# First units of block 1: q's and k's weights in halves, modulation sums rearranged, extra matmuls on TensorE

## The chip, the cores and the metric

The kernel runs on one core of one Trainium2 chip. The metric is device time in microseconds (us) of one execution; the kernel before takes 1196.93 us (median of three runs).

## The reference, cut to what matters

Two transformer blocks on 256 tokens of width 1024, all in float32. The change lies in the first 100 us, in the head of block 1:

```python
mod = jax.nn.silu(c) @ w_ada + b_ada                 # (1024) @ (1024, 6144)
sh1, sc1, ga1, sh2, sc2, ga2 = jnp.split(mod, 6)
h = modulate(rms_norm(x, g_norm1), sh1, sc1)         # h * (1 + sc1) + sh1
z = h @ w_in                                         # (256, 1024) @ (1024, 5120)
q, k, v, xb, bg, cg, gates = jnp.split(z, splits)
```

Behind it come rotary attention, a gated convolution, output rows, a mixture of 32 experts, and a second block.

## The kernel before

**Products.** Each matrix is split in two float32r parts, a lead (ScalarE: copy) and a rest (original minus lead), and every product is three matmuls: lead x lead, lead x rest, rest x lead. `row_products` issues such a triple for one of 8 contraction tiles k of 128 rows, for 128 tokens and 512 columns. A unit such as `q0` is 8 triples (24 matmuls) in one PSUM bank. `channel_tiles` makes the units of xb, cg and bg: 16 triples of 256 tokens.

**Weights.** A weight chunk (2 MB: 8 contraction tiles x 512 columns) comes by DMA into one of six ring slots. SyncE (SP) issues all of them in the order of `loads1`, and waits before each for the unit that last used the slot (`holds`). ScalarE then writes the leads in two halves of 2048 elements a partition (`lead_weights`, L1550), VectorE the rest of the first half (`rest_weights`, L1992), GpSimd the rest of the second half in two quarters (L814). GpSimd's queue runs through the chunks in order, and issues eleven small loads (`small_loads`) behind v's rests.

**Head.** c is turned into columns (`cT`). The modulation sums g1a and g1b are each 2 halves of 16 matmuls over 2 MB of `w_ada` (`modulation_half`, L902): g1a gives shift and scale for contraction tiles 0 to 3, g1b for 4 to 7. ScalarE copies the sums (`modulation_sums`, L1599), TensorE makes columns of them (`half_columns`, L947 and L948, 8 matmuls of 2 moving columns), ScalarE copies these (L1614), VectorE makes the scales (`first_scales`). Beside it, x is squared (L1559), VectorE forms the row factors and writes xn (L2038), and TensorE transposes xn (L892). Then h is made by contraction tile: `h1_fulls` (L2076) and `h1_rests` (L2085) on VectorE, `h1_leads` (L1620) on ScalarE; q's products follow.

**Late sums.** g2 (4 chunks of 2 MB, `late_pair`, L912, all in slot 4) follows behind the units named in `PAIR_AT`; each chunk's load waits for the sum before it. VectorE and ScalarE work strictly in program order: VectorE forms the rests of k and v, then `head_norm` of q (L1931 to L1949), adds g2_1, forms xb's rest, adds g2_2, then `head_norm` of k, whose transposes (`tk`, L959) TensorE needs behind xb1. ScalarE adds g2_0 (L1599) ahead of v's leads, and writes xb's leads before it copies v0 out.

Of the kernel before, what the change touches and what calls it, by code (L numbers as in the profile page):

```python
# [13 lines left out]
P = 128  # L14
# [26 lines left out]
COL = 512  # L41
# [92 lines left out]
def two_blocks(nc, A, consts, out):  # L134
    with ExitStack() as ctx:
# [179 lines left out]
        dense_order = ["g1a", "g1b"] + UNITS1 + [f"pa{t}{h}" for t, h in TH] + [f"pb{t}{h}" for t, h in TH]  # L315
# [20 lines left out]
        PAIR_AT = {"q1": ("g2", 0), "k1": ("g2", 1), "v1": ("g2", 2), "xb1": ("g2", 3)}  # L336
        PAIR_AT.update({f"gate{n}0": ("g3", n) for n in range(4)})
        ROW_AT = {"cg0": 4, "cg1": 5, "bg0": 10, "bg1": 11}
# [4 lines left out]
        small_order = ["cT", "params", "xt00", "xt10", "cols_g1a", "xt01", "xt11", "cols_g1b"]  # L343
# [51 lines left out]
        dense_released = {"g1a": (sem("acc_copied"), 1), "g1b": (sem("acc_copied"), 2)}  # L395
# [24 lines left out]
        small_released = {"cT": (sem("c_ready"), 1), "params": (sem("pcol_ready"), 1), "rsb": (sem("rsb_ready"), 1),  # L420
# [85 lines left out]
        def ada_half(group, n, slot):  # L506

            loads = []
            for at, c in enumerate(ADA_GROUPS[group]):
                src = w_ada[4 * n * P:4 * (n + 1) * P, c * COL:(c + 1) * COL].rearrange("(k p) n -> p k n", p=P)  # L510
                loads.append((four_of(slot)[:, :, at * COL:(at + 1) * COL], src))
            chunk(f"{group}_{n}", slot, loads, after(group) if n else (sem("ada_pairs"), 1 + (group == "g1b")))
# [11 lines left out]
        def columns_in(name):  # L524
            slot = ROT1[ROT_NAMES.index(name) % 3]
            weights(name, slot, [(wide(slot), cols(w_in, IN1[name] * COL))], name + "1")
# [3 lines left out]
        columns_in("q")  # L530
        ada_half("g1b", 0, 4)
        ada_half("g1b", 1, 0)
        columns_in("k")
# [140 lines left out]
        def halves(m):  # L674

            size, slot = split_size[m], slot_of[split_chunks[m]]
            out = []
            for a in range(0, size, HALF_SLOT):
                b = min(a + HALF_SLOT, size)
                out.append((ring[:, slot, a:b], ring_r[:, slot, a:b], lead_home(m)[1][:, a:b]))  # L680
            return out

        lead_done = [0]
        for m in range(len(split_chunks)):
            lead_done.append(lead_done[-1] + len(halves(m)))

        ON_DVE = {M[name] for name in ("q", "fk", "fv", "hi", "hg", "gate_b0")}
        rest_dve, rest_pool = [0], [0]
        for m in range(len(split_chunks)):
            rest_dve.append(rest_dve[-1] + 1 + (m in ON_DVE))  # L690
            rest_pool.append(rest_pool[-1] + (0 if m in ON_DVE else 2 * (len(halves(m)) - 1)))

# [31 lines left out]
        def _(sp_):  # L724
# [5 lines left out]

            sp_.dma_start(cst[:, 0:C_FIRST], consts[:, 0:C_FIRST]).then_inc(sem("first_in"), 16)
            for name in loads1:
                load(name)
# [3 lines left out]
                if name == "g1a_0":  # L737
                    sp_.dma_start(x[:, :, :], A["x"][0].rearrange("(t p) d -> p t d", p=P)).then_inc(sem("x_in"), 16)
# [52 lines left out]
        def _(pool):  # L791
# [15 lines left out]
            def rest_weights(m):  # L807

                if len(halves(m)) == 2 and m not in ON_DVE:
                    w, rest, lead = halves(m)[1]  # L810
                    pool.wait_ge(sem("w_lead"), lead_done[m + 1])
                    for a in (0, HALF_SLOT // 2):
                        b = a + HALF_SLOT // 2
                        nc.gpsimd.tensor_tensor(rest[:, a:b], w[:, a:b], lead[:, a:b].bitcast(F32),  # L814
                                                ALU.subtract).then_inc(sem("w_rest_b"), 1)
# [18 lines left out]
        def _(pe):  # L834
# [8 lines left out]
            def weights_ready(m, at):  # L843

                if at < HALF_SLOT or m in ON_DVE:
                    pe.wait_ge(sem("w_rest_a"), rest_dve[m] + 1 + (at >= HALF_SLOT))
                else:
                    pe.wait_ge(sem("w_rest_b"), rest_pool[m] + 1 + (at >= HALF_SLOT + HALF_SLOT // 2))
# [180 lines left out]

            pe.wait_ge(sem("first_in"), 16)  # L1030
# [6 lines left out]
            pe.wait_ge(sem("params_in"), 16 * (len(PARAM_ROWS) - 1))  # L1037
            o = small.claim(pe, "params")
            nc.tensor.transpose(o[:, 0:PARAM_N], prow[0:PARAM_N, :], ident[0:PARAM_N, 0:PARAM_N]).then_inc(small.done, 1)
            modulation_half("g1a", 1, g1a).then_inc(dense.done, 1)  # L1040

            def h1_ready(t, k):
                return sem("h1_rest"), KD * (k // 4) + 4 * t + k % 4 + 1

            for t, h in XT:
                pe.wait_ge(sem("xn_ready"), t + 1)
                transposes(f"xt{t}{h}", xn[:, t, :], h)
                if (t, h) == (1, 0):
                    half_columns("g1a")
            g1b = dense.claim(pe, "g1b")  # L1050
            q_rows = [dense.claim(pe, f"q{t}") for t in range(TT)]
            for k in range(4):
                row_products(q_rows[0], M["q"], 0, k, h1_ready)
            modulation_half("g1b", 0, g1b).then_inc(sem("ada_pairs"), 1)
            for k in range(4):
                row_products(q_rows[1], M["q"], 1, k, h1_ready)
                if k == 1:
                    modulation_half("g1b", 1, g1b).then_inc(dense.done, 1)
            half_columns("g1b")
            for t in range(TT):  # L1060
                for k in range(4, KD):
                    last = row_products(q_rows[t], M["q"], t, k, h1_ready)
                last.then_inc(dense.done, 1)

            for name in UNITS1:
                chunk_name, u = name[:-1], int(name[-1])
                if chunk_name == "q":
                    pass
                elif chunk_name in ("xb", "cg", "bg"):
# [428 lines left out]
        def _(act_):  # L1498
# [44 lines left out]
            def lead_weights(m, parts=(0, 1)):  # L1543

                if 0 in parts:
                    arrived(act_, split_chunks[m])
                    act_.wait_ge(*lead_holds(m))
                for n, (w, _, lead) in enumerate(halves(m)):
                    if n in parts:
                        af(lead, w, ACT.Copy).then_inc(sem("w_lead"), 1)  # L1550
# [36 lines left out]
            af(pcol[:, :], src[:, 0:PARAM_N], ACT.Copy).then_inc(sem("pcol_ready"), 1)  # L1587
# [35 lines left out]
            modulation_sums("g1a")  # L1623
            normed_columns(0, 0)
            normed_columns(1, 0)
            half_columns(0)
            lead_weights(0, (0,))
            h1_leads(0, 0)
            normed_columns(0, 1)
            normed_columns(1, 1)  # L1630
            h1_leads(1, 0)
            lead_weights(0, (1,))
            act_.wait_ge(sem("lb_sub_ready"), 1)
            af(lbt[:, 2:4, :], lbt[:, 0:2, :], ACT.Exp).then_inc(sem("lb_exp_ready"), 1)
            modulation_sums("g1b")
            half_columns(1)
            h1_leads(0, 1)
            h1_leads(1, 1)

            for unit in UNITS1:  # L1640
                name, u = unit[:-1], int(unit[-1])
                if u == 0:
                    lead_weights(M[name] + 1)
# [107 lines left out]
            for unit in UNITS2:  # L1751
                name, u = unit[:-1], int(unit[-1])
                if u == 0 and name != "fq":
                    lead_weights(M[name] + 1, (1,) if name == "hq" else (0, 1))
# [128 lines left out]
        def _(dve):  # L1883
# [101 lines left out]
            def rest_weights(m, parts=(0, 1)):  # L1985

                for n in range(2 if m in ON_DVE else 1):
                    if n not in parts:
                        continue
                    w, rest, lead = halves(m)[n]  # L1990
                    dve.wait_ge(sem("w_lead"), lead_done[m] + 1 + n)
                    v.tensor_tensor(rest, w, lead.bitcast(F32), ALU.subtract).then_inc(sem("w_rest_a"), 1)  # L1992
# [47 lines left out]
            def lower_bounds_differences():  # L2040
                dve.wait_ge(sem("pcol_ready"), 1)
# [19 lines left out]
            def first_scales(h):  # L2061
# [3 lines left out]
                dve.wait_ge(sem("pcol_ready"), 1)  # L2065
# [21 lines left out]

            first_scales(0)
            h1_fulls(0, 0)
            rest_weights(0, (0,))  # L2090
            h1_rests(0, 0)
            h1_fulls(1, 0)
            h1_rests(1, 0)
            lower_bounds_differences()
            rest_weights(0, (1,))
            lower_bounds()
            link(v.tensor_copy(rs[:, 9, :], rs[:, 0, :]))
            first_scales(1)
# [501 lines left out]
```

## Time and profile before

| | |
|---|---|
| runs | 1193.87, 1196.93, 1198.81 us; median 1196.93 |
| profiled execution, span | 1196.8 us |
| TensorE busy, share of the span | 96% |
| mean granted TensorE clock | 0.989 |
| DMA over the span | 277 GB/s |
| DMA from 359 to 718 us (the experts) | about 421 GB/s |

The profiled execution has no time of its own beside its span, which stands 0.1 us from the median. A busy TensorE is not one at full speed: at half the granted clock each matmul lasts about twice as long, and the expert stage keeps it busy at the pace of its transfers.

### The profile page before, as it was taken

What the parts mean: (1) busy time and instruction counts of PE and PEld (TensorE: products, weight loads), DVE (VectorE), ACT (ScalarE), POOL (GpSimd) and SP (SyncE); (2) the same over time, 40 slices, a digit from 0 to 9 for tenths busy, and PEclk for the clock granted to TensorE, in tenths of its full rate; (3) what the DMA queues carried; (4) which work ended last, traced back from release to release, by engine and by line L of the source; (5) the groups of instructions that cost most, each with busy time, mean ns of one, the idle gap of its engine ahead of it and who ended that gap; (6) DMA issues with size and microseconds to landing.
All of it is one profiled execution on the core that took longest, in us unless ns stands there. A gap on an engine that the chain in (4) does not pass through costs nothing.

```text
span 1196.8 us, 15588 instructions
## 1 busy us (share of the span) xinstructions
PE 1148.5 (96%) x5930; PEld 761.6 (64%) x5930; DVE 481.1 (40%) x971; ACT 410.5 (34%) x609; POOL 222.0 (19%) x100
## 2 busy tenths in 40 slices
PE   4999999999999999999989998999999999999998
PEld 2678867774444444444434435978877788888886
DVE  3475552753222222222212215589454653323226
ACT  3533454232111111111111115664245363444334
POOL 0163333300000000000000002200313444443522
PEclk8899999999999999999999998999999999999999
DMA  9897366689899999999999996453223464645541
GB/s 355 322 329 264 128 229 246 269 329 367 339 377 421 423 422 421 422 422 422 422 420 421 422 421 240 160 192 126 86 71 141 150 194 159 210 147 181 201 163 48
DMA packets 92329, 331.68 MB, mean 277 GB/s; under 512 B 3937, under 2 KB 26754, under 8 KB 66674
## 3 DMA queue, kind: packets, MB, share of 16 engines
q1 hardware_dynamic: 91648, 330.36, 71.2%
q0 software_dynamic: 432, 0.48, 0.2%
q8 instruction: 40, 0.66, 0.2%
q14 instruction: 15, 0.12, 0.0%
q10 hardware_dynamic: 194, 0.06, 0.0%
HBM read 329.84 MB, written 1.05 MB: 276 GB/s over the span
## 4 chain that ended last, share of the span: by engine, by line
PE 73%; DMA 16%; DVE 6%; issue 2%; ACT 2%; SPq 0%; DVEq 0%; ACTq 0%
DMA ring<-in_w 15%; PE ps L839 14%; PE ps L840 13%; PE ps L841 13%; PE ps L1196 13%; PE ps L1238 5%; PE ps L1168 1%; PE ps L1169 1%; DVE ring_r L1992 1%; PE ps L912 1%; DMA ring<-in_w_ada 1%; ACT ring_r L1550 1%; PE ps L1349 1%; PE ps L976 1%; PE ps L974 1%
## 5 line engine op out<-in xcount | busy, mean ns | idle before, releaser
L814 POOL TENSOR_TENSOR ring_r<-ring,ring_r 128x1024 fp32r<-128x1024 f32 x76 | 197.8, 2623 | 824.5 <-ACT ring_r L1550 824.4
L1196 PE MATMUL ps<-ring,arena 128*64 128x512 f32 x1008 | 226.0, 596 | 8.8 <-DMA ring<-in_w 7.7
L840 PE MATMUL ps<-ring_r,hl_r 128*128 128x512 f32 x528 | 211.4, 400 | 0.0
L839 PE MATMUL ps<-ring_r,hl_r 128*128 128x512 f32 x480 | 197.5, 411 | 10.7 <-DVE hr_r L2085 6.1
L841 PE MATMUL ps<-ring_r,hr_r 128*128 128x512 f32 x480 | 192.0, 400 | 0.0
L1550 ACT ACTIVATE ring_r<-ring 128x2048 fp32r<-128x2048 f32 x90 | 167.4, 1907 | 62.5 <-PE ps L841 45.0
L1196 PEld LDWEIGHTS ps<-ring,arena 128*64 128x64 f32 x1008 | 69.5, 137 | 149.0 <-issue 127.6
L1992 DVE TENSOR_TENSOR ring_r<-ring,ring_r 128x2048 fp32r<-128x2048 f32 x52 | 121.3, 2339 | 84.5 <-ACT ring_r L1550 84.3
L839 PEld LDWEIGHTS ps<-ring_r,hl_r 128*128 128x128 f32 x480 | 91.8, 191 | 41.2 <-issue 14.7
L840 PEld LDWEIGHTS ps<-ring_r,hl_r 128*128 128x128 f32 x528 | 101.0, 191 | 21.9
L841 PEld LDWEIGHTS ps<-ring_r,hr_r 128*128 128x128 f32 x480 | 91.8, 191 | 22.3
L1238 PE MATMUL ps<-ring,arena 128*64 128x512 f32 x448 | 100.9, 604 | 0.7 <-ACT arena L1715 0.7
L1715 ACT ACTIVATE arena<-ps 128x512 f32<-128x512 f32 x16 | 9.6, 598 | 185.1 <-PE ps L1224 185.1
L1238 PEld LDWEIGHTS ps<-ring,arena 128*64 128x64 f32 x448 | 31.3, 138 | 59.1 <-issue 57.3
L1721 ACT ACTIVATE hl_r<-hl 128x512 fp32r<-128x512 f32 x32 | 20.1, 630 | 119.4 <-DVE hl L2307 119.4
L1168 PE MATMUL ps<-arena_r,ya_r 128*128 128x128 f32 x256 | 60.2, 280 | 0.5 <-DVE flagf L2260 0.5
L1168 PEld LDWEIGHTS ps<-arena_r,ya_r 128*128 128x128 f32 x256 | 49.2, 192 | 13.6 <-issue 13.5
L2293 DVE COPY arena<-ps 64x1 f32<-64x1 f32 x32 | 5.0, 156 | 121.8 <-PE ps L1204 121.3
L2307 DVE SCALAR_TENSOR_TENSOR hl<-ps,arena,ga2b 128x512 f32<-128x512 f32 x32 | 23.9, 748 | 68.9 <-PE ps L1238 68.9
L2300 DVE TENSOR_TENSOR arena<-arena,ps 128x512 f32<-128x512 f32 x16 | 11.0, 688 | 92.9 <-PE ps L1196 92.9
L839 PE MATMUL ps<-hl_r,ring_r 128*128 128x256 f32 x160 | 45.8, 286 | 0.0
L840 PE MATMUL ps<-hr_r,ring_r 128*128 128x256 f32 x160 | 45.1, 282 | 0.0
(370 smaller groups left out, 1650.7 us busy)
## 6 DMA issues: line engine op xcount, KB each, us to landing
ring<-in_w SPq DMA_DIRECT2D x91, 2048.0 KB, 21.5
ring<-in_w_in SPq DMA_DIRECT2D x21, 2048.0 KB, 8.4
ring<-in_w_ada SPq DMA_DIRECT2D x16, 1024.0 KB, 10.2
ring<-in_w_ffn_gate SPq DMA_DIRECT2D x11, 1024.0 KB, 5.2
ring<-in_w_ffn_up SPq DMA_DIRECT2D x11, 1024.0 KB, 7.8
ring<-in_w_ffn_down SPq DMA_DIRECT2D x5, 2048.0 KB, 7.8
ring<-in_w_ada SPq DMA_DIRECT2D x4, 2048.0 KB, 8.7
ring<-in_w_o SPq DMA_DIRECT2D x2, 2048.0 KB, 7.7
```

The lines of the kernel that those rows point to most:

```text
L814: nc.gpsimd.tensor_tensor(rest[:, a:b], w[:, a:b], lead[:, a:b].bitcast(F32), ALU.subtract).then_inc(sem("w_rest_b"), 1)
L839: mm(o, lhsT=a_lead, rhs=b_lead, start=start, stop=False, skip_group_check=True)
L840: mm(o, lhsT=a_lead, rhs=b_rest, start=False, stop=False, skip_group_check=True)
L841: return mm(o, lhsT=a_rest, rhs=b_lead, start=False, stop=stop, skip_group_check=True)
L912: last = mm(o[32 * i:32 * i + 32, :], lhsT=cpad[:, 2 * n + k, :], rhs=w[:, k, i * COL:(i + 1) * COL], start=start and k == 0, stop=stop an ...
L1168: mm(into, lhsT=xp_l[:, t, k, :], rhs=S_r[:, t, :], start=t == 0, stop=False)
L1196: last = mm(H[slots_of(e), :], lhsT=xs[:, k, slots_of(e)], rhs=w, start=k == 0, stop=k == KD - 1)
L1238: last = mm(Y[slots_of(e), :], lhsT=hidT[:, f, slots_of(e)], rhs=w2_rows(e, f, half, early), start=f == 0, stop=f == FT - 1)
L1550: af(lead, w, ACT.Copy).then_inc(sem("w_lead"), 1)
L1721: af(ys_l[:, cols_], ys[:, cols_], ACT.Copy).then_inc(sem("moe_ys_lead"), 1)
L1992: v.tensor_tensor(rest, w, lead.bitcast(F32), ALU.subtract).then_inc(sem("w_rest_a"), 1)
L2307: v.scalar_tensor_tensor(ys[:, cols_], Y, place_w, ga2b[:, cols_], ALU.mult, ALU.mult).then_inc(sem("moe_ys_scaled"), 1)
```

## The change

- SP: x is loaded ahead of everything but the small table. q's and k's chunks are split; their first halves (contraction tiles 0 to 3) are issued between the 1 MB pieces of g1b_0 (q upper, piece, k upper, piece). Then come g1b_1, q's second half, k's second half.
- Leads: q's are written in quarters, k's in halves of their own. q's rests are four quarters on VectorE; k's first half goes to GpSimd, its second half to VectorE.
- TensorE: 9 matmuls without use (`keep_warm`, float32, 128x256) behind `cT`; the transposes of xn stand before g1a_0 (one unit) and before g1a_1 (three units); `half_columns` of g1a follows g1a_1; then 3 more `keep_warm`; the first halves of q0 and q1; g1b_0; first half of k0; g1b_1; two triples of k1; `half_columns` of g1b; the rest of k1's first half; q's second halves; g2_0; k's second halves.
- g2_1 to g2_3 stand behind v0, xb0 and cg0 (before: k1, v1, xb1), the rows of `modulation_row` one unit later.
- VectorE adds g2_1 behind xb's rest, g2_2 behind cg's rest, g2_3 in the attention loop.

```diff
-        PAIR_AT = {"q1": ("g2", 0), "k1": ("g2", 1), "v1": ("g2", 2), "xb1": ("g2", 3)}
+        PAIR_AT = {"q1": ("g2", 0), "v0": ("g2", 1), "xb0": ("g2", 2), "cg0": ("g2", 3)}
...
+            if m == M["q"]:
+                return [(a, a + QUARTER, "dve") for a in range(0, SLOT, QUARTER)]
+            if m == M["k"]:
+                return [(0, QUARTER, "pool"), (QUARTER, HALF_SLOT, "pool"), (HALF_SLOT, SLOT, "dve")]
...
             sp_.dma_start(cst[:, 0:C_FIRST], consts[:, 0:C_FIRST]).then_inc(sem("first_in"), 16)
+            sp_.dma_start(x[:, :, :], A["x"][0].rearrange("(t p) d -> p t d", p=P)).then_inc(sem("x_in"), 16)
             for name in loads1:
-                load(name)
+                if name == "g1b_0":
+                    upper_half("q")
+                    (view, src), second = chunks[name]
+                    sp_.dma_start(view, src).then_inc(chunk_in[slot_of[name]], 16)
+                    upper_half("k")
+                    sp_.dma_start(*second).then_inc(chunk_in[slot_of[name]], 16)
+                else:
+                    load(name)
...
+            def keep_warm(n):
+
+                for _ in range(n):
+                    mm(dense.bank("k0")[:, 0:C_FIRST], lhsT=ident, rhs=cst[:, 0:C_FIRST], start=True, stop=True)
...
+            keep_warm(9)
+            pe.wait_ge(sem("params_in"), 16 * (len(PARAM_ROWS) - 1))
+            o = small.claim(pe, "params")
+            nc.tensor.transpose(o[:, 0:PARAM_N], prow[0:PARAM_N, :], ident[0:PARAM_N, 0:PARAM_N]).then_inc(small.done, 1)
+            normed_transposes(XT[0:1])
             pe.wait_ge(sem("cpad_ready"), 1)
             g1a = dense.claim(pe, "g1a")
             modulation_half("g1a", 0, g1a).then_inc(sem("ada_pairs"), 1)
...
+            normed_transposes(XT[1:])
             modulation_half("g1a", 1, g1a).then_inc(dense.done, 1)
...
+            half_columns("g1a")
+            keep_warm(3)
             q_rows = [dense.claim(pe, f"q{t}") for t in range(TT)]
...
+            for t in range(TT):
+                half_rows(q_rows[t], "q", t, 0)
+            g1b = small.claim(pe, "g1b")
             modulation_half("g1b", 0, g1b).then_inc(sem("ada_pairs"), 1)
...
+            k_rows = [dense.claim(pe, f"k{t}") for t in range(TT)]
+            half_rows(k_rows[0], "k", 0, 0)
+            modulation_half("g1b", 1, g1b).then_inc(small.done, 1)
+            for k in range(2):
+                row_products(k_rows[1], M["k"], 1, k, h1_ready)
             half_columns("g1b")
+            for k in range(2, 4):
+                row_products(k_rows[1], M["k"], 1, k, h1_ready)
             for t in range(TT):
...
+                half_rows(q_rows[t], "q", t, 1).then_inc(dense.done, 1)
+            late_pair(*PAIR_AT["q1"])
+            for t in range(TT):
+                half_rows(k_rows[t], "k", t, 1).then_inc(dense.done, 1)
```

## Rows read from the trace of the kernel before

**Rows 1.** The page, part 1: busy time of the engines.
```profile
PE 1148.5 (96%) x5930; PEld 761.6 (64%) x5930; DVE 481.1 (40%) x971; ACT 410.5 (34%) x609; POOL 222.0 (19%) x100
```

**Rows 2.** Windows of 10 us: busy us of each engine, granted clock, DMA share, GB/s.
```profile
40.00:50.00 10.00, 7.51 (x32) 6.28 (x31) 5.61 (x19) 6.63 (x11) 0.00 (x0) 0.66 1.03 399
60.00:70.00 10.00, 10.00 (x52) 6.73 (x51) 9.48 (x16) 1.62 (x3) 10.00 (x9) 1.00 0.89 308
110.00:120.00 10.00, 10.00 (x82) 9.53 (x81) 4.97 (x15) 4.84 (x7) 0.00 (x0) 1.00 0.60 209
```

**Rows 3.** Windows of 1 us, the same columns: where clock and DMA change.
```profile
15.00:16.00 1.00, 0.00 (x0) 0.00 (x0) 0.73 (x5) 0.26 (x3) 0.00 (x0) 0.89 1.05 387
...
22.00:23.00 1.00, 1.00 (x9) 1.00 (x8) 0.00 (x0) 0.73 (x2) 0.00 (x0) 0.70 1.05 387
...
26.00:27.00 1.00, 0.00 (x0) 0.00 (x0) 0.71 (x3) 1.00 (x3) 0.00 (x0) 0.51 1.05 387
...
32.00:33.00 1.00, 1.00 (x5) 0.76 (x3) 0.61 (x1) 0.46 (x2) 0.00 (x0) 0.58 1.05 385
...
43.00:44.00 1.00, 0.00 (x0) 0.00 (x0) 0.78 (x4) 0.45 (x2) 0.00 (x0) 0.54 1.02 406
...
49.00:50.00 1.00, 1.00 (x4) 0.81 (x3) 1.00 (x1) 1.00 (x1) 0.00 (x0) 0.54 1.05 387
...
52.00:53.00 1.00, 1.00 (x9) 0.54 (x7) 0.00 (x0) 0.00 (x0) 1.00 (x1) 1.00 0.04 16
```

**Rows 4.** Timeline of TensorE, 0 to 100 us: start, us, line, what, idle before and releaser.
```profile
9.40 3.37 PE L902 MATMUL ps<-ring,cpad 128*32 128x512 f32 x16 [6.16 <-DMA ring<-in_w_ada]
...
17.37 3.64 PE L902 MATMUL ps<-ring,cpad 128*32 128x512 f32 x16 [4.36 <-DMA ring<-in_w_ada]
20.95 1.88 PE L892 MATMUL ps<-cst,ya 128*128 128x128 f32 x8
...
29.10 0.79 PE L839 MATMUL ps<-ring_r,hl_r 128*128 128x512 f32 x1 [3.66 <-DVE hr_r L2085]
...
37.23 1.92 PE L902 MATMUL ps<-ring,cpad 128*32 128x512 f32 x16
...
44.92 0.80 PE L839 MATMUL ps<-ring_r,hl_r 128*128 128x512 f32 x1 [2.48 <-DVE hr_r L2085]
...
52.98 1.92 PE L912 MATMUL ps<-ring,cpad 128*32 128x512 f32 x16
...
66.27 1.92 PE L912 MATMUL ps<-ring,cpad 128*32 128x512 f32 x16
...
81.55 0.38 PE L839 MATMUL ps<-hl_r,ring_r 128*128 128x256 f32 x1
...
95.67 1.09 PE L959 MATMUL ps<-cst,arena 128*128 128x128 f32 x8 [1.47 <-DVE arena L1949]
```

**Rows 5.** Timeline of ScalarE: first square, one lead half, xb's leads.
```profile
11.94 0.63 ACT L1559 ACTIVATE spp<-x 128x512 f32<-128x512 f32 x1 [8.23 <-DMA x<-in_x]
...
24.61 1.91 ACT L1550 ACTIVATE ring_r<-ring 128x2048 fp32r<-128x2048 f32 x1
...
69.57 3.73 ACT L1550 ACTIVATE ring_r<-ring 128x2048 fp32r<-128x2048 f32 x2 [2.60 <-DMA ring<-in_w_in]
```

**Rows 6.** Timeline of VectorE: xn, rest of q's first half, head_norm of q begins.
```profile
17.71 1.42 DVE L2038 TENSOR_SCALAR ya<-x,rs 128x1024 f32<-128x1024 f32 x2
...
26.55 2.29 DVE L1992 TENSOR_TENSOR ring_r<-ring,ring_r 128x2048 fp32r<-128x2048 f32 x1 [0.28 <-ACT ring_r L1550]
...
59.61 3.42 DVE L1931 TENSOR_TENSOR spp<-arena 128x1024 f32<-128x1024 f32 x1
```

**Rows 7.** Timeline of GpSimd: v's quarters, xb's quarters.
```profile
59.25 6.04 POOL L814 TENSOR_TENSOR ring_r<-ring,ring_r 128x1024 fp32r<-128x1024 f32 x2 [3.79 <-ACT ring_r L1550]
...
73.39 5.75 POOL L814 TENSOR_TENSOR ring_r<-ring,ring_r 128x1024 fp32r<-128x1024 f32 x2 [0.37 <-ACT ring_r L1550]
```

**Rows 8.** Timeline of SP: issue of g2_1's load; xb's follows it.
```profile
54.96 0.88 SPq L729 DMA_DIRECT2D ring<-in_w_ada  x2
```

More of the change, by code:

```diff
@@ L672, in chunk_done @@
             return (sem("down_chunks"), int(name[4:]) + 1) if name != "down5" else after("down11")
[L674 to L680, printed above, removed]
-            return out
-        lead_done = [0]
+        QUARTER = HALF_SLOT // 2
+        ON_DVE = {M[name] for name in ("fk", "fv", "hi", "hg", "gate_b0")}
@@ L688, in two_blocks, with lead_of @@
[L688 to L691, printed above, removed]
+            for n, (_, _, by) in enumerate(rest_pieces(m)):
+                rested[by] += 1
+                rest_at[m, n] = sem(dict(dve="w_rest_a", pool="w_rest_b")[by]), rested[by]
+        def lead_of(m, b):
+            return sem("w_lead"), lead_at[m, [n for n, (_, end) in enumerate(lead_pieces(m)) if b <= end][0]]
@@ L807, in rest_weights @@
             def rest_weights(m):
[L809 to L815, printed above, removed]
+                for a, b, by in rest_pieces(m):
+                    if by == "pool":
+                        w, rest, lead = piece(m, a, b)
+                        pool.wait_ge(*lead_of(m, b))
+                        nc.gpsimd.tensor_tensor(rest, w, lead.bitcast(F32), ALU.subtract).then_inc(sem("w_rest_b"), 1)
             for m in range(M["fq"]):
@@ L1541, in two_tiles, with lead_weights @@
                 return t[:, 2 * u:2 * u + 2, :]
[L1543 to L1550, printed above, removed]
+            led = [0]
+            def lead_weights(m, parts=None):
+                for n in range(len(lead_pieces(m))) if parts is None else parts:
+                    a, b = lead_pieces(m)[n]
+                    if split_chunks[m] in upper_halves and b <= HALF_SLOT:
+                        act_.wait_ge(sem(f"{split_chunks[m]}_upper_in"), 16)
+                    else:
+                        arrived(act_, split_chunks[m])
+                    if n == 0:
+                        act_.wait_ge(*lead_holds(m))
+                    led[0] += 1
+                    assert lead_at[m, n] == led[0]
+                    w, _, lead = piece(m, a, b)
+                    af(lead, w, ACT.Copy).then_inc(sem("w_lead"), 1)
             squares = [0]
@@ L1983, in pair, with rest_weights @@
                 return src.rearrange("p (j t) -> p j t", t=T)
[L1985 to L1992, printed above, removed]
+            rests = [0]
+            def rest_weights(m, parts=None):
+                for n, (a, b, by) in enumerate(rest_pieces(m)):
+                    if by == "dve" and (parts is None or n in parts):
+                        rests[0] += 1
+                        assert rest_at[m, n][1] == rests[0]
+                        w, rest, lead = piece(m, a, b)
+                        dve.wait_ge(*lead_of(m, b))
+                        v.tensor_tensor(rest, w, lead.bitcast(F32), ALU.subtract).then_inc(sem("w_rest_a"), 1)
             def gated_a(tag, t, h):
```

153 lines of the change are left out of this document (84 added, 69 removed).

## The prediction

> **What bounds the kernel now.** I read first the busy times, then windows over the head of block 1, then TensorE's timeline and what released it, then the queues beside it. TensorE is busy 96% of the span [rows 1], so a gain must come from where it idles or runs at half clock. In the head it does both: between 40 and 50 us it is busy 7.51 of 10 us at a mean clock of 0.66 [rows 2]. It waits for g1a_1's load until 17.37, for h until 29.10 (3.66 us) and again until 44.92 (2.48 us) [rows 4]. The granted clock falls from full to half (2.4 to 1.2 GHz) near 15.8, rises near 22.6, falls at 26.0, rises near 32.9, falls at 43.1, rises near 49.9 [rows 3]. TensorE had worked for 5.2, 3.8 and 5.0 us before the rises; the falls at 26.0 and 43.1 came 0.6 us after its work ended (29.10 - 3.66, 44.92 - 2.48), with transposes and two-column products just before [rows 4]. The 1.00 that the windows give ahead of 15 us I do not believe: the half of g1a at 9.40 lasts 3.37 us, near the 3.64 us at half clock and not the 1.92 us at full [rows 4]. From 44.92 to 100 us TensorE waits once, 1.5 us for `head_norm` of k at 95.67 [rows 4]. DMA is saturated at 385 to 399 GB/s until 52 us, then nearly idle [rows 2, 3]; later it has room (share 0.60, [rows 2]) until the experts.
>
> **What the head can give.** The transfers set arrivals. At 388 GB/s 1 MB (2^20 bytes) takes 2.7 us. g1a_0 landed at 9.40; x, one such MB earlier, lands near 6.8, where it landed at 11.94 [rows 4, 5]. Then, with the same bytes ahead, g1a_1 at 17.4 as before, q upper 20.1, g1b_0 28.2, k upper between them, g1b_1 33.6, q lower 36.3, k lower 39.0, table and g2_0 47, v 52.3. v can't come sooner by reordering: all bytes ahead of it stay.
>
> **Step 1, to the end of g1a_1 (call it X; before 17.37 + 3.64 = 21.0).** From x's landing to the first half of xn took 17.71 + 0.71 - 11.94 = 6.5 us [rows 5, 6], so xn0 is ready at 13.3. The 9 useless matmuls start near 3.3. No row shows one. The nearest are the modulation halves, float32 too: two rounds of four products side by side, 512 columns in 3.37 / 2 = 1.69 us at half clock and 0.96 at full [rows 4], so 0.84 or 0.48 for 256 columns. Nine end between 7.6 and 10.9, before 13.3; nothing waits for them, and I price them at nothing. Were xn there first, what remained of them would be the price. But then TensorE idles some 3 us, what it idled before the fall at 15.8 (from 12.8, [rows 3, 4]), so I expect the clock low again at 13.3 to 15. Then: 4 transposes 0.9, g1a_0 3.6, 12 transposes at 0.235 (1.88 / 8) at half clock and half that at full, g1a_1. With the clock rising 4 to 5 us after 13.3, g1a_1 runs from 19.5 and X = 21.4. Bounds: clock never lost, g1a_1 starts on landing, X = 17.4 + 1.9 = 19.3; late rise, 22.4.
>
> **Step 2, X to the first product.** Before 29.10 - 21.0 = 8.1. Out of it go 1.0 (transposes stood between the sum's copy and the columns), half of q's rest (2.29 / 2 = 1.15, [rows 6]) and its wait of 0.3 for the lead: 5.7. q upper (20.1) is there. First product at X + 5.7 = 27.1, 2.0 sooner than before.
>
> **Step 3, first product to the end of g1b_1 (Y; before 37.23 + 1.92 = 39.1).** Now 24 products of q, 12 of k and two halves stand here, before 18 of q and the halves. A product costs 0.235 us at full clock (k's 48 run from 54.83 to 66.27, two gaps included) and 0.43 at half. 36 x 0.235 + 2 x 1.95 + 0.3 (q's second quarter comes 0.3 late on VectorE) = 12.7. k's upper quarters on GpSimd: behind the scales at X + 3.2 ScalarE writes four leads of h (1.6), q's second quarter (1.0), four leads of h, k's half (1.9, [rows 5]), so GpSimd begins at X + 9.3 and has them at 2.9 each [rows 7] by X + 12.2 and X + 15.1; TensorE wants them at X + 13.6 and X + 15.0. They are just covered by q's products and g1b_0; without that cover they would cost up to 5.8. Half clock at the first product costs 1.7 more (nine products, as from 29.10 on, less what waits absorb); the 3 `keep_warm` may or may not prevent it, I take 0.9. Y = 21.4 + 5.7 + 12.7 + 0.9 = 40.7: 1.6 later than before, though more is done.
>
> **Step 4, Y to the end of g2_0.** Two triples (1.4), columns (1.9), two triples: Y + 4.7. The columns are out at Y + 3.3, scales 0.65 later, then four fulls (1.1) and the first rest (0.3): h's second half begins at Y + 5.35 (before Y + 5.8), so the wait of 2.48 shrinks to 0.7 and the clock should hold, which also saves the 12 slow products behind 44.92, 2.3 us. q's last quarter is formed behind h's rests, by Y + 6.4 + 1.15, and wanted at Y + 6.75: 0.8 of stall. 24 products: Y + 11.8. g2_0 (landed 47): Y + 13.7 = 54.4. Before: 52.98 + 1.92 = 54.9. Then k needs only 24 products, to 60.1, where before k ended at 66.2.
>
> **Step 5, where the lead of 6 us meets GpSimd.** ScalarE adds g2_0 and only then writes v's leads; v's rests, eleven small loads and xb's rests follow each other on GpSimd. From the end of g2_0 to the last of xb's quarters this took 73.39 + 5.75 - 54.9 = 24.2 us [rows 7]. xb's own load is chained to g2_0 as well: issued at 54.96, in at 69.57, leads written at 73.3, 0.1 before the quarters start [rows 5, 7, 8]. None of this is shortened. I add 0.5, because `head_norm` of k now falls on xb's quarters (beside v's quarters L1931 took 3.42 us, and the quarters 6.04 against 5.75, [rows 6, 7]). So xb is whole at 54.4 + 24.7 = 79.1. TensorE wants that quarter, without waits, at 60.1 + 5.65 + 0.4 + 1.95 + 5.65 (v0, a short wait for v's last quarter, g2_1, v1) + 2.2 = 75.9. It waits 3.2 us, in two pieces. Before it wanted it at 81.55 + 2.2 = 83.8, 4.6 us after it was ready: the cover is used up. Of the 83.8 - 79.1 = 4.7, 1.95 is g2_2, which now follows xb0: 2.75 gained.
>
> **Step 6, to cg0.** `head_norm` of k now starts at about 74 instead of 82.3 and is done near 86, TensorE wants it at 90.5: the wait of 1.5 (1.6 with its start) goes. Moved with their SP issues, g2_2, cg, g2_3 and bg land 3 us or more before their use, as bg waits behind g2_2 only in SP's queue; rows and late sums cost the same wherever they stand.
>
> **Sum:** 2.75 + 1.6 = 4.4 us. Behind cg0 loads are released by TensorE's own progress and DMA has room, so the lead passes on to the experts' stream, which starts sooner by as much. 1196.8 - 4.4 = 1192.4; the span stands 0.1 from the median, so 1192.5. Less than the 6 us (0.5%) that a measurement of this kernel can tell from no change, with runs 4.9 us apart.
>
> Every microsecond on Y moves the end by one, down to Y = 38: below that v's landing at 52.3 holds ScalarE.
>
> **Rivals.**
> A. *The clock is kept from the first useless matmuls on.* For it: TensorE has fed gaps. Against: 3 us idle ahead of 13.3. X = 19.3, Y = 37.7, g2_0's end 51.4, lead on v's load 52.3 instead of 52.0: 4.4 + 3.0 - 0.3 = 7.1 gained, 1189.8. If besides GpSimd's chain shows slack that I do not see (xb's load quicker because the small loads meet another transfer), up to the 3.2 of step 5 more: 1186.6.
> B. *Transposes don't lift the clock.* In the trace the clock rose in the 22nd microsecond, with transposes running but 3.6 us of modulation just before [rows 3, 4]; in the change the same stands before the 12 transposes, which the forecast follows. If the clock does not rise there: 12 x 0.235, g1a_1 3.64, X = 24.2, and half clock at the first product: Y = 24.2 + 5.7 + 12.7 + 1.7 = 44.3, gain 0.8: 1196.1. The Trainium skill reports (TensorE: Matmul & The Clock Gate, Part 4: PE-mode transpose) that the full clock does not engage for transposes as it does for products; by that rule this rival is the outcome, and the rise at 22.6 speaks against it without settling it.
> C. *Slower: the clock stays low through q's and k's products.* Each costs 0.19 more, and the new order has waits inside (q's second quarter, columns, last quarter). 23 more slow ones eat the gain, 55 make it 0.5% slower; with all 96 slow it is 18 us, 1210. Against: no row shows more than about 12 in a row slow [rows 3, 4].
> D. *Nothing moves*, since xb's load is slowed by the small loads (60 to 70 us ran at 308 GB/s, [rows 2]) by another 3.5, or the clock falls during the wait at xb0: 1196.
>
> **Chances.** Forecast 0.48 (own range 1190 to 1195), A 0.24, B 0.12, C 0.05, D 0.11. The range 1187 to 1197 takes in A but for its last part, B and D, and leaves C and more than 10 us of gain out. Faster by over 0.5% (below 1191): A and a fifth of the forecast, 0.34. Slower (above 1202.9): 0.05. Within: 0.61.
>
> **What would show it.** x's squares near 6.8; the end of g1a_1 near 21.4; first product near 27; the half g1b_1 ends near 40.7; a wait of 0.7 instead of 2.48 ahead of q's second half; full clock from 44 to 50; GpSimd at work on xb until 79, and TensorE waiting for it in xb0 for about 3 us; no wait ahead of `tk`. The prediction is wrong if the clock holds at 13 to 17 us (too slow), or if TensorE's wait moves to a load.

## The result, and the profile after

| | median of the runs | range | runs |
|---|---|---|---|
| before | 1197.47 us | 1193.46 to 1200.09 | 20 |
| changed kernel | 1193.81 us | 1191.8 to 1197.6 | 20 |

The ratio is 0.9976, 95% interval 0.9967 to 0.9985: about 2.9 us of 1197 by the ratio, 3.7 by the medians. The change is slightly faster, by less than the 0.5% set as the bound of "same". The prediction said 1192.5 us and gave "within 0.5%" 0.61.

Two things about the numbers ahead of the prediction were not seen then. A run's time is its profiled span plus 1.8 to 2.0 us, in each kernel below (1197.6 against 1195.8 here), so the span of before, 1196.8, belongs to the run of 1198.81, the slowest of the three; it does not stand 0.1 from their median as the text said. And the profiled run of the changed kernel is the slowest of its 20, so I also use a second profiled run of the same program (label a_again, 1194.19 us, span 1192.4), which is near the median.

Part 1 of the page of the changed kernel, the run of 1197.6 us:

```profile
PE 1153.5 (96%) x5954; PEld 766.2 (64%) x5954; DVE 483.1 (40%) x973; ACT 411.0 (34%) x611; POOL 221.3 (19%) x100
```

TensorE has 24 instructions more than in [rows 1], all of `keep_warm` (12 matmuls, two records each), and its busy share is the same; the gain isn't seen here but in where the idle time lies. TensorE's timeline of this run (start, us, line, what, idle time before it and its releaser):

```profile
3.12 6.65 PE L1068 MATMUL ps<-cst 128*128 128x256 f32 x18
...
13.32 0.66 PE L927 MATMUL ps<-cst,ya 128*128 128x128 f32 x4 [1.96 <-DVE ya L2104]
13.91 1.92 PE L937 MATMUL ps<-ring,cpad 128*32 128x512 f32 x16
15.77 1.53 PE L927 MATMUL ps<-cst,ya 128*128 128x128 f32 x12
17.48 1.92 PE L937 MATMUL ps<-ring,cpad 128*32 128x512 f32 x16 [0.18 <-DMA ring<-in_w_ada]
...
25.46 0.50 PE L877 MATMUL ps<-ring_r,hl_r 128*128 128x512 f32 x1 [0.44 <-DVE hr_r L2151]
...
36.52 1.92 PE L937 MATMUL ps<-ring,cpad 128*32 128x512 f32 x16
...
43.73 0.50 PE L877 MATMUL ps<-ring_r,hl_r 128*128 128x512 f32 x1 [0.52 <-DVE hr_r L2151]
46.09 0.47 PE L877 MATMUL ps<-ring_r,hl_r 128*128 128x512 f32 x1 [0.68 <-DVE ring_r L2058]
50.46 1.92 PE L947 MATMUL ps<-ring,cpad 128*32 128x512 f32 x16
...
78.19 0.55 PE L877 MATMUL ps<-hl_r,ring_r 128*128 128x256 f32 x1 [5.29 <-DVE ring_r L2058]
```

The head is shorter than forecast: g1a_1 starts as its load lands and X is 19.4, the first product comes at 25.46 against 29.10 before [rows 4], the wait of 2.48 us ahead of q's second half is 0.52 + 0.68, and g2_0 ends at 52.4 with half of k done. Then 5.29 us are lost ahead of xb's products, and the releaser is VectorE. VectorE's timeline of the same run:

```profile
69.60 0.29 DVE L2012 TENSOR_TENSOR arena<-spp 128x128 f32<-128x128 f32 x1
69.81 8.23 DVE L2058 TENSOR_TENSOR ring_r<-ring,ring_r 128x2048 fp32r<-128x2048 f32 x1
77.97 0.68 DVE L2125 TENSOR_TENSOR acc<-ps,acc 128x512 f32<-128x512 f32 x1
```

And GpSimd's, v's quarters and xb's:

```profile
57.43 6.02 POOL L853 TENSOR_TENSOR ring_r<-ring,ring_r 128x1024 fp32r<-128x1024 f32 x2 [23.73 <-ACT ring_r L1609]
...
71.19 4.69 POOL L853 TENSOR_TENSOR ring_r<-ring,ring_r 128x1024 fp32r<-128x1024 f32 x2
```

The rest of xb's first half, 2.29 us long elsewhere, has a record of 8.23 us and ends 2.16 us after GpSimd's two quarters (71.19 + 4.69 = 75.88). It started while GpSimd still issued its small loads (until 71.19), and what lies behind the quarters is just the time that it needs elsewhere. The quarters ran in 2.35 us each: GpSimd wasn't slowed, VectorE stood still. TensorE idles meanwhile, and in windows of 1 us the granted clock falls (columns as in [rows 2]):

```profile
76.00:77.00 1.00, 0.00 (x0) 0.00 (x0) 1.00 (x1) 0.00 (x0) 0.00 (x0) 0.74 0.82 317
77.00:78.00 1.00, 0.00 (x0) 0.00 (x0) 1.00 (x2) 0.00 (x0) 0.00 (x0) 0.50 1.00 387
...
83.00:84.00 1.00, 1.00 (x10) 1.00 (x9) 0.90 (x4) 0.00 (x0) 0.00 (x0) 0.85 0.07 14
```

Eight triples of xb0 take 0.64 us instead of 0.36, 2.2 us more. So g3_0, the first late sum that stands at the same place in both kernels, starts at 141.59, 0.8 us ahead of before (142.38), and the span is 1.0 shorter.

In the second run VectorE keeps its pace and GpSimd is stretched. VectorE's timeline of a_again:

```profile
70.28 2.29 DVE L2058 TENSOR_TENSOR ring_r<-ring,ring_r 128x2048 fp32r<-128x2048 f32 x1
...
73.08 2.82 DVE L1994 TENSOR_TENSOR spp<-arena 128x1024 f32<-128x1024 f32 x1
```

GpSimd's timeline of it, xb's quarters:

```profile
71.65 6.46 POOL L853 TENSOR_TENSOR ring_r<-ring,ring_r 128x1024 fp32r<-128x1024 f32 x2
```

And the list of TensorE's waits from 54 to 150 us (us in total, times, longest):

```profile
PE ps L877 <- POOL ring_r L853: 4.0, 4, 2.3
```

The four pieces in TensorE's timeline of a_again, for v's last quarter, xb's third and last, and cg's last:

```profile
64.06 0.47 PE L877 MATMUL ps<-ring_r,hl_r 128*128 128x512 f32 x1 [0.49 <-POOL ring_r L853]
...
74.97 0.36 PE L877 MATMUL ps<-hl_r,ring_r 128*128 128x256 f32 x1 [0.17 <-POOL ring_r L853]
78.25 0.36 PE L877 MATMUL ps<-hl_r,ring_r 128*128 128x256 f32 x1 [2.33 <-POOL ring_r L853]
...
94.77 0.36 PE L877 MATMUL ps<-hl_r,ring_r 128*128 128x256 f32 x1 [0.99 <-POOL ring_r L853]
```

xb is whole at 78.1 by either road; here its first three quarters come earlier, TensorE waits 2.5 us for it in two pieces, as step 5 of the prediction has it (3.2 forecast), and its clock stays full (1.00 in each window from 76 to 79). No wait stands ahead of `tk`, but one of 0.99 us, which wasn't forecast, ahead of cg's last quarter. g3_0 starts at 138.45, 3.9 us ahead of before, and the span is 4.4 shorter. That equals the sum that was forecast, but its parts don't: up to the end of g2_0 the gain is 1.36 us (forecast 0.5), from there to g3_0 2.57 (forecast 3.9), behind g3_0 0.5 (forecast nothing). That they add up to the forecast is in part luck.

### The profile page after: what moved, and what is told of

The parts are those of the page before. It is cut to its first block, busy times and chain, and to the rows that moved or that the text cites. A ratio compares the mean times of both kernels' runs of the same rounds, so it can differ in the third digit from the quotient of the medians.

```text
span 1195.8 us, 15643 instructions
## 1 busy us (share of the span) xinstructions
PE 1153.5 (96%) x5954; PEld 766.2 (64%) x5954; DVE 483.1 (40%) x973; ACT 411.0 (34%) x611; POOL 221.3 (19%) x100
## 4 chain that ended last, share of the span: by engine, by line
PE 71%; DMA 17%; DVE 7%; issue 2%; ACT 2%; SPq 0%; DVEq 0%; ACTq 0%
DMA ring<-in_w 15%; PE ps L877 13%; PE ps L878 13%; PE ps L879 13%; PE ps L1247 13%; PE ps L1289 5%; DVE ring_r L2058 2%; PE ps L1219 1%; PE ps L1220 1%; DMA ring<-in_w_in 1%; DMA ring<-in_w_ada 1%; ACT ring_r L1609 1%; PE ps L1400 1%; PE ps L947 1%; PE ps L1011 1%
## 5 line engine op out<-in xcount | busy, mean ns | idle before, releaser
L1609 ACT ACTIVATE ring_r<-ring 128x2048 fp32r<-128x2048 f32 (+1 forms) x92 | 167.9, 1870 | 80.7 <-PE ps L879 44.7
L2058 DVE TENSOR_TENSOR ring_r<-ring,ring_r 128x2048 fp32r<-128x2048 f32 (+1 forms) x54 | 127.6, 2368 | 94.0 <-ACT ring_r L1609 93.7
L1219 PEld LDWEIGHTS ps<-arena_r,ya_r 128*128 128x128 f32 x256 | 49.2, 192 | 13.6 <-issue 13.5
```

What stands on the lines that cost most here:

```text
L1219: mm(into, lhsT=xp_l[:, t, k, :], rhs=S_r[:, t, :], start=t == 0, stop=False)
```

## The experiments

Twelve runs followed, of the changed kernel and nine edited ones, in three groups, each group beside the kernel before on one chip. Three readings of each profiled run split its span: the end of g2_0 (what the head does), from there to the start of g3_0 (what the stretch behind it does), and from there to the end. Before: 54.9, 87.5 and 1054.5.

| label | median us (runs) | ratio to before, 95% | profiled span | g2_0 ends | to g3_0 | g3_0 to the end | TensorE's waits, 54 to 150 us |
|---|---|---|---|---|---|---|---|
| changed kernel | 1193.81 (20) | 0.9976 [0.9967, 0.9985] | 1195.8 | 52.4 | 89.2 | 1054.2 | VectorE 5.3, GpSimd 1.1 |
| a_again | 1194.19 (5) | 0.9963 [0.9949, 0.9976] | 1192.4 | 53.5 | 84.9 | 1053.9 | GpSimd 4.0 |
| loads_late | 1193.26 (5) | 0.9962 [0.9948, 0.9976] | 1195.5 | 52.4 | 90.4 | 1052.7 | VectorE 3.6 and 1.9, GpSimd 1.1 |
| xb_dve | 1191.18 (5) | 0.9947 [0.9934, 0.9961] | 1192.6 | 56.5 | 84.7 | 1051.4 | GpSimd 1.9, ScalarE 1.7 |
| xb_dve_again | 1193.76 (7) | 0.9967 [0.9955, 0.9978] | 1191.4 | 53.6 | 84.5 | 1053.3 | GpSimd 1.9, ScalarE 1.6 |
| both | 1191.84 (5) | 0.9956 [0.9942, 0.9969] | 1188.6 | 53.7 | 81.5 | 1053.4 | GpSimd 0.7 |
| both_again | 1191.11 (6) | 0.9949 [0.9935, 0.9963] | 1189.5 | 56.2 | 81.5 | 1051.8 | GpSimd 0.5 |
| both_nowarm | 1193.42 (12) | 0.9965 [0.995, 0.998] | 1191.1 | 55.3 | 81.5 | 1054.4 | GpSimd 0.7 |
| both_pairs | 1195.03 (8) | 0.9975 [0.9963, 0.9988] | 1193.7 | 55.0 | 84.4 | 1054.4 | DMA 2.0, VectorE 0.3 |
| no_warm | 1196.52 (12) | 0.9987 [0.9974, 1.0001] | 1195.6 | 55.9 | 84.2 | 1055.5 | GpSimd 3.3 |
| pool_after | 1194.49 (12) | 0.9975 [0.9963, 0.9987] | 1191.6 | 55.1 | 83.9 | 1052.5 | GpSimd 3.2 |
| pairs_old | 1193.98 (12) | 0.997 [0.9956, 0.9985] | 1192.8 | 53.4 | 86.6 | 1052.8 | DMA 4.9 |
| before_xb | 1198.39 (11) | 1.0004 [0.9995, 1.0012] | 1196.7 | 55.1 | 87.6 | 1053.9 | VectorE 1.5, DMA 0.2 |

The part behind g3_0 is the same work in every kernel, yet its time lies between 1051.4 and 1055.5, a spread of 4.1 us that no edit explains. Most of it goes with falls of the granted clock that some runs have and others don't. Between 713 and 723 us the clock falls to 0.50 for about 3 us in seven of the fourteen profiled runs, and these are the seven whose last part takes 1053.9 or more. In xb_dve and both_again, 1051.4 and 1051.8, the fall that the others have between 728 and 740 is missing as well. In no_warm the clock is also at half from 254 to 260, and its last part is the longest. The window 716 to 717 us of a_again:

```profile
716.00:717.00 1.00, 1.00 (x6) 0.38 (x4) 0.00 (x0) 0.00 (x0) 0.00 (x0) 0.50 1.04 403
```

and of xb_dve:

```profile
716.00:717.00 1.00, 0.43 (x4) 0.24 (x2) 0.00 (x0) 0.53 (x1) 0.00 (x0) 1.00 0.96 401
```

So whole spans of two kernels, one profiled run each, can't be compared to better than some 4 us; the readings up to g3_0 can.

**a_again.** The changed kernel, unedited.

> The changed kernel once more, nothing altered. Theory 1 (its gain is eaten in xb0): VectorE's rest of xb's first half, 2.29 us of work, lasts about 8 us again because GpSimd works beside it, TensorE waits about 5.3 us for it and then makes eight triples at half clock (2.2 us more). The time is about 3 us under the kernel before. Rival (a chance of the one profiled execution): the rest lasts 2.3 us this time, TensorE waits about 3 us or less for GpSimd's last quarter as predicted, and the span is several us shorter than 1195.8.

The median stays at 1194, and the profiled run had no 8-us record, as the rival on record has it: the collision at xb (both engines at work on its rests at once) goes either way from run to run. Of the 20 runs of the changed kernel 13 lie between 1191.8 and 1194.3 and seven between 1195.66 and 1197.6; pool_after below shows that this split can't be put down to the collision alone.

**xb_dve, xb_dve_again.** GpSimd no longer has anything of xb.

```diff
-        ON_DVE = {M[name] for name in ("fk", "fv", "hi", "hg", "gate_b0")}
+        ON_DVE = {M[name] for name in ("xb", "fk", "fv", "hi", "hg", "gate_b0")}
```

> xb's second half is formed on VectorE as well, in one piece behind the first; GpSimd keeps only its small loads there. Rival 1b: the first rest ends by 72.2 and the second by 74.5, TensorE waits nothing or under 1 us at xb0 and keeps its clock: 7.5 us won there, of which cg's late landing (84.5) takes back about 4 at cg0, so some 3 to 4 us under the changed kernel. Theory 1a: the first rest is held until the small loads end near 71.2, so it ends near 73.4 and the second at 75.7, wait 0.5 to 1. If instead neither engine's work matters (the rest waits for a transfer): the first rest again ends near 78, no gain, or a loss of 2 us by the second half.

> The changed kernel with xb's rests wholly on VectorE, a second time, beside the kernel of the next label on one chip. Theory: 1191.2 again, 6 us below before, ratio near 0.995. Rival (the first result was luck of the clock in the head): 1194, as the changed kernel.

The medians, 1191.2 and 1193.8, are 2.6 us apart, and the intervals of the ratios barely touch. The second is what the rival forecast (1194, as the changed kernel), so at the median no gain of this edit is shown; what holds in both is the trace up to g3_0. Both halves of xb take VectorE 4.49 us, and TensorE doesn't wait at xb0, yet the stretch behind g2_0 is hardly shorter than in a_again (84.5 against 84.9). The wait has moved on to `tk` and cg0 (where a_again waited 0.99 us already). TensorE's timeline of xb_dve_again:

```profile
90.23 0.66 PE L994 MATMUL ps<-cst,arena 128*128 128x128 f32 x4 [1.58 <-ACT arena L1587]
94.44 0.36 PE L877 MATMUL ps<-hl_r,ring_r 128*128 128x256 f32 x1 [1.36 <-POOL ring_r L853]
```

Both waits come from cg: its load lands at 85.49, where ScalarE begins cg's leads ahead of the copy that `tk` needs, and GpSimd starts cg's quarters at 89.29. ScalarE's timeline of xb_dve_again:

```profile
85.49 3.72 ACT L1609 ACTIVATE ring_r<-ring 128x2048 fp32r<-128x2048 f32 x2 [11.41 <-DMA ring<-in_w_in]
```

The same row of both, whose g2_0 ended within 0.1 us of it:

```profile
82.47 3.72 ACT L1609 ACTIVATE ring_r<-ring 128x2048 fp32r<-128x2048 f32 x2 [8.32 <-DMA ring<-in_w_in]
```

cg's load was issued at 68.62 and 68.69: 16.9 us against 13.8 with the eleven small loads out of its way.

**loads_late, both, both_again.** `small_loads` stands behind cg's rests in GpSimd's queue instead of behind v's; both adds this to xb_dve.

```diff
-                if m == M["v"]:
+                if m == M["cg"]:
```

> GpSimd issues its eleven small loads behind cg's rests instead of behind v's. Theory 1a (the small loads are what holds VectorE's rest and slows cg's load): xb's first rest starts near 69.8 and ends by 72.1, xb's quarters on GpSimd from 69.5 to 75, cg lands near 80 instead of 84.5; TensorE's wait in xb0 shrinks from 5.3 to 1 or 2 us without loss of clock: about 5 us under the changed kernel. Rival 1b (it is GpSimd's quarters that hold it, two tensor operations on two engines): the rest still ends only behind the quarters, near 76.5, the wait stays at 3.5 us or more, and the gain over the changed kernel is 1 to 2 us.

> Both edits: small loads behind cg's rests and all of xb's rests on VectorE. Under either form of theory 1 nothing holds VectorE at xb, cg lands near 80, and TensorE has no wait from q's second half to cg0: 7 us under the changed kernel, about 10 under the kernel before (0.8%). If the lead is lost elsewhere (behind cg0, or in the experts, whose transfers set the pace), the trace has no wait in xb0 but the time stays within 2 us of the changed kernel.

> The same with the eleven small loads behind cg's quarters besides. Theory: the small loads cost nothing once GpSimd no longer forms xb's rests, and moving them gains nothing: 1191 to 1192, the same as the kernel with xb on VectorE alone. Rival: their place ahead of cg's load is worth 1 us or more: 1190 or less.

Alone it is no gain (1193.3 against 1194.2 on the same chip, ratios 0.9962 and 0.9963). GpSimd starts xb's quarters earlier (69.41), and in the profiled run VectorE stands still again, over two instructions of its timeline:

```profile
69.66 2.37 DVE L2012 TENSOR_TENSOR arena<-spp 128x128 f32<-128x128 f32 x1
71.96 4.45 DVE L2058 TENSOR_TENSOR ring_r<-ring,ring_r 128x2048 fp32r<-128x2048 f32 x1
```

The first is 0.29 us long elsewhere, and the second ends 2.15 us after GpSimd's quarters (69.41 + 4.85 = 74.26). No small load was being issued then, so of the two readings on record it is GpSimd's quarters that hold VectorE, not the small loads. cg lands at 80.47, but bg, now beside the small loads, 18.0 us after its issue (87.75 to 105.76) instead of 13.3 (85.80 to 99.09 in a_again), and TensorE waits 1.9 us for a sum. With xb on VectorE too, the stretch behind g2_0 is 81.5 us in all three profiled runs of that form (both, both_again, both_nowarm): 3.4 less than in a_again, and what is left of waits is 0.5 to 0.7 us. That is what GpSimd's queue, xb's rests and the small loads together, costs the changed kernel when VectorE keeps its pace: about the 2.5 us at xb0 and the 0.99 at cg0 (3.2 was forecast, for xb0 alone). The medians are 1191.8 and 1191.1, 2.4 us below a_again in the first group, where I had expected 7. Of both_again I had expected that moving the small loads adds nothing; the median is 2.65 us below xb_dve_again, near the 3.0 that the traces show between 84.5 and 81.5. In the first group, though, both stands 0.7 above xb_dve, so what moving the small loads adds is shown in the traces and not at the median.

**before_xb.** The kernel before, with xb's second half on VectorE (the same set of names in its code).

> The kernel before with one edit: the second half of xb's rests is formed by VectorE instead of GpSimd. Theory (GpSimd's chain bounds only once the head's lead has used up the cover): before, TensorE wanted that quarter 4.6 us after it was ready and never waited for it, and VectorE was idle for 7 us behind xb's first rest, so the edit gives nothing here: 1198, within 1 us of the kernel before, with the wait of about 1.5 us ahead of the transposes of k still there. Rival (it is the sharing between VectorE and GpSimd that costs time everywhere, head or no head): 2 to 4 us faster here too.

Nothing gained, the wait ahead of `tk` unchanged at 1.5. So GpSimd's chain costs time only once the head leads: the rival that VectorE and GpSimd lose time to each other everywhere falls.

**pool_after.** GpSimd begins xb's quarters only when VectorE has the first half.

```diff
+                        if m == M["xb"]:
+                            pool.wait_ge(*rest_of(m, 0))
```

> GpSimd's quarters of xb wait for VectorE's rest of xb's first half, so that the two never meet there. Theory (who gets the memory first is a matter of chance, and the 8.23 us come from losing it): the rest lasts 2.3 us in the profile, TensorE waits 3 to 4 us for the last quarter and keeps its clock, and the runs' upper values (above 1195) become rare; the median is 0.5 to 1.5 us under the changed kernel. Rival (the rest is held by something else than the quarters, such as the small loads): it again lasts some 5 to 8 us in some runs, and because the quarters now follow it the time is worse by up to 4 us.

The collision is gone from the trace (the quarters run 74.24 to 79.91, behind VectorE), TensorE waits 3.2 us, and the stretch is 83.9. But the median didn't move from the changed kernel's, where I had expected 0.5 to 1.5 us less, and five of its 12 runs are above 1195, up to 1197.46. So the collision of these pieces is not the only thing that makes a run slow.

**no_warm, both_nowarm.** Both `keep_warm` calls removed, from the changed kernel and from both.

> The changed kernel without its twelve matmuls of no use. Theory (every microsecond lost in the head moves the end by one, as g2_0's sum starts the chain to xb's last quarter): the clock is at half at g1a_1, which ends near 21 instead of 19.4, and in the first products too; k ends 2 to 3 us later and the time is 1.5 to 3 us above the changed kernel, close to the kernel before. Rival (the chain behind xb has slack, or the clock rises by itself before g1a_1): k's end moves but the time stays within 0.5 us of the changed kernel.

> Small loads behind cg's rests, xb's rests all on VectorE, and no useless matmuls. With no wait at xb0 to hide in, what the head loses goes through: 3 us above the kernel with both edits if the useless matmuls keep the clock, within 0.5 us of it if they don't.

The clock was at half through g1a_0 in the profiled run of no_warm (3.64 us), X is 21.4 and the first product waits 3.2 us; g2_0 ends at 55.9. The ratio, 0.9987, has 1 in its interval, against 0.9963 and 0.9976 with the extra matmuls; 0.9965 against 0.9949 and 0.9956 in the other pair. By the ratios the extra matmuls are worth 1.1 to 2.9 us, but the intervals overlap in each of the four pairings, and the kernels with and without them ran in different groups. The traces don't place this gain: with them g2_0 ended between 52.4 and 56.5 in ten profiled runs, without them at 55.3 and 55.9. That they help is likely and not shown.

**pairs_old, both_pairs.** g2_1 to g2_3 back behind k1, v1 and xb1, with the changed head.

```diff
-        PAIR_AT = {"q1": ("g2", 0), "v0": ("g2", 1), "xb0": ("g2", 2), "cg0": ("g2", 3)}
+        PAIR_AT = {"q1": ("g2", 0), "k1": ("g2", 1), "v1": ("g2", 2), "xb1": ("g2", 3)}
```

> Only the places of g2_1, g2_2 and g2_3 go back behind k1, v1 and xb1. Theory (GpSimd's chain sets xb0's end): v0 and v1 come 1.9 us later, TensorE waits 1.9 us less at xb0, and the pair behind xb0 is gone: about 1.9 us under the changed kernel, and cg lands 7 us sooner. Rival (the places are right, since a pair behind k1 would wait for its load): g2_1 has been asked for at 52.4 and can't land before 58.5, so TensorE idles about 1 us behind k1 and nothing is won.

> Both edits, and g2_1 to g2_3 back behind k1, v1 and xb1. Theory: the pair behind k1 still finds its load 2 us late, and the one behind v1 too, with a spell of half clock, so it ends 2 to 3 us above the kernel with both edits: 1194. Rival (the small loads, now out of the way, were what made the pairs' loads late): the same as that kernel, 1191 to 1192.

TensorE's waits in pairs_old, 54 to 150 us:

```profile
PE ps L947 <- DMA ring<-in_w_ada: 4.9, 2, 2.6
```

TensorE's timeline of both_pairs, g2_1:

```profile
62.80 2.56 PE L947 MATMUL ps<-ring,cpad 128*32 128x512 f32 x16 [2.01 <-DMA ring<-in_w_ada]
```

With k's products done sooner (59.2 in pairs_old, 66.3 before), a sum behind k1 finds its load missing. In pairs_old this took over the idle time of GpSimd's wait (DMA 4.9, GpSimd 0; the clock fell for about 4 us at 77), so its median is that of the changed kernel; where GpSimd's wait is gone it costs 2.9 us of the stretch (84.4 against 81.5) and 3.9 of the median. So the new places of the late sums, which the prediction took to cost the same as the old ones, gain nothing at the median of the changed kernel, and keep the lead once GpSimd's wait is gone.

## Why the prediction was right, point by point

**Step 1 (X).** Forecast 21.4, bounds 19.3 and 22.4. Ten profiled runs of kernels with this head, `keep_warm` included, gave 19.2 to 22.1, the changed kernel's own two 19.4. The difference is the clock: xn was ready at 13.3 to 13.5 as forecast in all ten. In four of them (after, a_again, loads_late, pairs_old) the clock was kept, g1a_0 took 1.92 us, and g1a_1 started on landing or just behind it; in the other six g1a_0 took 2.85 to 3.64. The run of both_again took the forecast's course, TensorE's timeline:

```profile
13.37 1.12 PE L927 MATMUL ps<-cst,ya 128*128 128x128 f32 x4 [2.02 <-DVE ya L2104]
14.41 3.64 PE L937 MATMUL ps<-ring,cpad 128*32 128x512 f32 x16
17.98 2.09 PE L927 MATMUL ps<-cst,ya 128*128 128x128 f32 x12
20.00 1.92 PE L937 MATMUL ps<-ring,cpad 128*32 128x512 f32 x16
```

Its windows of 1 us at the rise of the clock:

```profile
18.00:19.00 1.00, 1.00 (x9) 1.00 (x6) 0.00 (x0) 0.00 (x0) 0.00 (x0) 0.50 1.04 383
19.00:20.00 1.00, 1.00 (x10) 0.83 (x8) 0.00 (x0) 0.86 (x2) 0.00 (x0) 0.92 1.05 385
```

The clock rose near 19.1, 1.1 us into twelve transposes, and in the changed kernel's own run it stayed full through the twelve at 15.77. The outcome of rival B, X = 24.2, came in no run. The Trainium skill (TensorE: Matmul & The Clock Gate, Part 4: PE-mode transpose) says that the full clock doesn't engage for transposes. As it stands this does not fit these runs, where the clock was full through twelve transposes or rose among them; but products of the modulation always stood just before, so whether transposes alone lift the clock isn't shown. "The prediction is wrong if the clock holds at 13 to 17" came true in both profiled runs of the changed kernel: for the head's first part its forecast failed, and rival A is what happened. A's gain was not kept.

**Step 2.** X + 5.7 forecast; 25.46 - 19.40 = 6.1 and 25.30 - 19.36 = 5.9. The half clock fell into this stretch (0.50 from 22 to 25 in the changed kernel).

**Step 3.** First product to Y, 12.7 plus 0.9: 13.0 and 14.3 (Y 38.4 and 39.6; forecast 40.7). In a_again the first products ran at half clock until 29.0, in the other run at full. Rival C's low clock ended there; in none of the ten runs were more than about 12 products of the head slow, where C needed 23 more than forecast. k's quarters, 28.98 + 4.72 = 33.7 on GpSimd, lay in the shade of q's products as forecast.

**Step 4.** Y to the end of g2_0: 13.7 forecast, 13.9 and 14.0 in the two runs. The two waits, 0.52 and 0.68 (0.70 in a_again), stand for the forecast 0.7 and 0.8.

**Step 5.** End of g2_0 to xb whole: 24.7 forecast, 78.11 - 53.53 = 24.6 in a_again, and 24.5 to 24.8 in no_warm, pool_after and pairs_old, in which VectorE kept its pace too: xb follows the end of g2_0 as forecast. TensorE's wait at xb0: 3.2 forecast, 2.5 measured in a_again. Missed was the other course: that VectorE's own rest of the first half can stand still behind GpSimd's quarters. It makes xb late as a whole rather than in quarters, TensorE idles 5.3 us at a stretch, and the clock falls for 2.2 us more: 4.3 us of stretch between the two profiled runs (89.2 against 84.9). The second branch of rival D, that the clock falls during the wait at xb0, is what this run did; D didn't say why the wait would be long enough. The term that was mis-sized for this course is step 5's 0.5 us for the sharing of the two engines: it measured 0.7 in a_again (the quarters took 6.46 instead of 5.75), and in the other run 5.9 (VectorE's record of 8.23 instead of 2.29). Why VectorE's record starts 1.4 us ahead of the quarters that it stood still for, the trace doesn't show.

**Step 6.** The wait ahead of `tk` is gone in both runs, and no load is late for a moved sum. The prediction called DMA nearly idle behind 52 us, against its own row (308 GB/s from 60 to 70 us, [rows 2]). It looked at cg's load and not at its rests: cg lands at 85.79 in a_again, GpSimd has its last quarter at 94.6, and TensorE waits 0.99 us for it.

**Sum.** 4.4 forecast; spans 1.0 and 4.4 shorter; medians 3.7 and 3.9 apart, beside their own kernels before. "Every microsecond on Y moves the end by one" held in part. In a_again g2_0 ended 0.9 us sooner than forecast and xb was whole 1.0 sooner, but the wait at cg0 then took 0.99; no_warm, whose g2_0 ended 2.3 us later than a_again's, started g3_0 1.7 later. In the other run g2_0 ended 2.0 sooner than forecast, and xb was whole only 1.1 sooner, since VectorE stood still. Rival A would have needed 7.1 of gain; its early X came with the fall of the clock at 22. Against the time itself the forecast is 1.3 low: 0.54 because the median of three runs of before, 1196.93, lay below that of 20, 1197.47, and 0.74 because the gain was 3.66 and not 4.4. That the prediction set a span equal to a time did no harm to the number: 1196.93 - 4.4 is 1192.5 as well.

**Open.** What decides from run to run whether the clock is kept at 13 us, and whether VectorE or GpSimd stands still at xb, wasn't settled; nor was why pool_after, without the collision, still has runs up to 1197.5, nor why the clock falls near 255, 718 and 735 us in some runs and not in others. How much of the head's gain is due to x's early load and how much to the halves of the weights wasn't separated.

## What to carry to other kernels

When a head gets faster, list for each engine's queue behind it the time at which its work is needed and the time it is ready: here the cover of GpSimd's chain was 4.6 us and the lead 6, and the cure was to give a piece to the engine that stood idle, together with moving eleven small loads off the next big load's way (either alone gained less in the trace). Compare profiled runs at a mark behind the stage that was changed, and not by their whole spans, which here differ by up to 4 us for other reasons. Ahead of a sum of terms of a few microseconds, take two profiled runs of a program whose runs spread by 5 us, and check how a span stands to its run's time.

## What the runs showed of the hardware

- **VectorE and GpSimd.** A subtraction with both inputs in SBUF on VectorE either kept its 2.29 us while GpSimd's two quarters took 6.46 instead of 4.7, or stood still until they had ended (records of 8.23, and 2.37 with 4.45 us) while the quarters took 4.69 and 4.85. No run showed a split in between at that place. The Trainium skill (SBUF — State Buffer, Who interferes with whom) says this: the shared port pair is an exclusive lock, VectorE instructions with two SBUF inputs contend with GpSimd's reads, and the one that issues first keeps it while the other fully blocks. The traces agree on the blocking. On the order they agree in part: in a_again VectorE's record is the first (70.28 against 71.65) and it keeps its pace, and in loads_late GpSimd's is (69.41 against 69.66) and VectorE stands still; but in the changed kernel's other run VectorE's record starts at 69.81, GpSimd's at 71.19, and GpSimd won, over both of its instructions.
- **Small loads.** Eleven small loads issued by GpSimd beside a 2 MB load let it land 16.9 instead of 13.8 us after its issue (cg in xb_dve_again and both); moved one chunk on, they did the same to bg (18.0 instead of 13.3).
- **Useless matmuls.** Nine float32 matmuls of 256 columns are 18 instructions and took 6.65 us, 0.74 each (0.63 to 0.79 over the ten profiled runs that have them), between the 0.48 and 0.84 worked out from the modulation halves.
- **The clock.** In the ten profiled runs with the same head it fell and rose at different times: g1a_0 took between 1.92 and 3.64 us, and g2_0 ended between 52.4 and 56.5 us. Behind g3_0 a fall of 3 to 4 us is there in some runs and missing in others, and most of the spread of 4.1 us of that part goes with it. The two together are as large as the spread of 5 us between runs of one program.
